# Row sums on VectorE beside the gates and outputs of two more groups, and row tiles spaced by the time that steps leave to transfers

## The chip, the core and the metric

One core of one Trainium2 chip runs the whole program. The metric is the device time of one execution in microseconds. All data are float32.

## What is computed

One layer of a hybrid backbone on 1280 tokens of width 1024: 256 context tokens and 1024 latent tokens. In the kernel they are ten chunks of 128 tokens. Cut to what matters, the layer is:

```python
h = rmsnorm(x) * (1 + sc1) + sh1
u, v, zb, q, k, rv, rg_f, rg_b, gm = split(h @ w_in)
merged = sig(ga) * gmlp(u, v) + sig(gb) * pool(zb) + sig(gc) * retention(q, k, rv, rg_f, rg_b)
x = x + gt1 * (merged @ w_out)
h2 = rmsnorm(x) * (1 + sc2) + sh2
# retrieval: 8 heads, 16 of 16384 experts for each token and head
top_s, top_i = top_k(h2 @ wq . subkeys, 16)      # both sides, then the 16 best of 256 sums
act = gelu(u_tab[expert] . h2);  wgt = softmax(best) * act
x = x + gt2 * sum_over_experts(wgt * v_tab[expert])
y = rmsnorm(x)
```

## The kernel before

**Row tiles.** A token needs 128 experts, so a chunk of 128 tokens needs 16384 of them. They are fetched in row tiles, 128 for each chunk and 1280 in all. A row tile is one indirect transfer, issued by GpSimd (L993), that gathers 128 rows of 8 KB from the table: the u half and the v half of 128 experts, 1 MB together. It fills one of 8 slots (6 at first). Row `R` then goes through the engines:

- VectorE multiplies the u half with the tokens and sums: the dot product (L1558).
- ScalarE, one row later (`ACT_LAG`), makes the gelu (L1033) and the weight (L1036), and scales a small folding matrix by it (`lhs`, L1044).
- TensorE, three rows later (`PE_LAG`), multiplies the v half with that matrix and adds to two banks of PSUM (L1289). The slot is free when this is done.

For *chained* rows the last two steps differ. ScalarE leaves out L1044. VectorE, two rows after the dot product (`VEC_LAG`), scales the v half by the weight and adds the previous row's result (L1570; L1567 for the first row of a run). TensorE takes the last of a run of 16 (`RUN`) only. A chained row's slot is free when VectorE has made the next row's sum, the last one's when TensorE has taken it.

**The other work.** Everything but the row tiles is the *front*, a list of steps in a fixed order. Each step carries a planned cost for TensorE, ScalarE and VectorE. After the modulation, stage 0 and group 0 (context tokens), the list has the retention and pooling of the latent tokens (stage 1), then groups of chunks: `GROUPS = ((0, 1), (2, 3), (4, 5, 6), (7, 8, 9))`. A group's steps are `v` and `u` (products for the spatial gating), `ga` (its gate), `mix`, `rg` and `gc` (retention and its gate), `gb` (pooling's gate), `tr`, `wo` (output product), and `h2a` to `h2c`. A product step is 8 pairs of 128x128 by 512 on TensorE with a planned cost of 7.0. Then comes the group's ranking: `wq` steps on TensorE, and `topa`, `topb`, `topc` steps on VectorE, which find the experts. Some of the `topb` and `topc` steps of a group stand between the `v`, `ga`, `rg` and `gc` steps of the next. In the list the last 35 steps are ranking steps of the last group, 33 of them `top` steps.

Weights come in units of 2 MB from SyncE's queue into two buffers. A step that is the first to use a unit has `ev.first` set. A group has 20 units: 4 for `v` and `u`, 12 from `ga` to `wo`, and 4 for `wq`.

**Placing the row tiles.** All engines read one list, `plan.events`, in which `merge` puts the row tiles between the steps. For each group of rows it takes the stretch of the front from the step that makes them ready to the one that makes the next group's ready, adds up the larger of the planned costs of each step (`wall`), and gives each step a due row in proportion to the sum so far. Row tiles are placed while they are due and ready. The rows of group 0 thus lie beside stage 1, group 1 and the start of its ranking, those of group 1 (256 to 511) beside group 2, and those of group 2 (512 to 895) beside group 3. The last group's rows (896 to 1279) start at the last 35 steps, one for every `LAST_PACE` = 2.9 of `wall`; what is left follows when the front is done, with nothing between. `row_of` and `ready` hold a row back until its experts are ranked: rows 608 and later wait for a step in the middle of group 3's `rg`.

`chains` makes the runs: rows `R` to `R + 15`, with `R` a multiple of 16, if all are placed from the end of group 0's ranking to the first `wq` of group 1. These are 144 rows.

Of the kernel before, what the change touches and what calls it, by code (L numbers as in the profile page):

```python
# [44 lines left out]
ROWS = P  # L45
NR = NC * ROWS
ACT_LAG, VEC_LAG, PE_LAG = 1, 2, 3
RUN = 16
DEEP = 12
RANK_LAG = 3  # L50
LAST_PACE = 2.9
STAGES = ((0, 1), tuple(range(CC, NC)))
GROUPS = ((0, 1), (2, 3), (4, 5, 6), (7, 8, 9))
ORDER = tuple(c for cs in GROUPS for c in cs)
# [45 lines left out]
def row_of(R):  # L100

    p, rr = divmod(R, ROWS)
    pair, g, qq = rr // 32, rr // 16 % 2, rr % 16
    return p, g, pair, pair * 16 + qq, 2 * pair + qq // 8
# [42 lines left out]
class Plan:  # L147
# [231 lines left out]
    def ranking(self, k):  # L379

        cs = GROUPS[k]
        n, pairs = len(cs), 4 * len(cs)
        heads = [(m, hd) for m in range(pairs) for hd in range(2)]
        sides, sums = iter(heads), iter(heads)
        behind = 0

        def top(part, m, hd):
            pair, i = divmod(m, n)
            ev = self.add("top" + part, g=k, i=m, h=2 * pair + hd, j=hd, c=cs[i], p=BASE[k] + i,
                          z=4 * BASE[k] + m, y=self.at["rank", k, m],  # L390
                          act=.8 * (hd == 0 and part == "c") + 2.4 * (hd == 1 and part == "b"), dve=3.0)
            if part == "b" and hd == 1 and m:
                before, ib = divmod(m - 1, n)
                ev.ready = (BASE[k] + ib, before)

        for m in range(RANK_LAG if k else 0):
            self.query(k, m)
            yield
        for m in range(pairs):
            if k and m + RANK_LAG < pairs + 2:  # L400
                self.query(k, m + RANK_LAG)
                yield
            for _ in range(2):
                top("a", *next(sides))
                behind += 1
                yield
                if k == 0 or behind > DEEP - 2:
                    at = next(sums)
                    for part in "bc":
                        top(part, *at)  # L410
                        yield
                    behind -= 1
            if k:
                at = next(sums)
                for part in "bc":
                    top(part, *at)
                    yield
                behind -= 1
        yield "scored"
        for at in sums:  # L420
            for part in "bc":
                top(part, *at)
                yield
        ev = self.add("gsm", g=k, z=4 * BASE[k] + pairs - 1, act=3.2, dve=.2)
        ev.ready = (BASE[k] + n - 1, 3)
        yield
# [39 lines left out]

    def merge(self):

        wall = [max(ev.cost) for ev in self.front]
        starts = [self.ready[BASE[k], int(len(cs) > 2)] for k, cs in enumerate(GROUPS)] + [len(self.front)]  # L470
        due = [0.0] * (len(self.front) + 1)
        for k, cs in enumerate(GROUPS):
            a, b = starts[k], starts[k + 1]
            total = sum(wall[a:b])
            rows = min(len(cs) * ROWS, total / LAST_PACE if k == len(GROUPS) - 1 else len(cs) * ROWS)
            spent = 0.0
            for n in range(a, b):
                spent += wall[n]
                due[n + 1] = BASE[k] * ROWS + rows * spent / total
        self.loaded, self.tail, self.x_at, self.gt_at, row = set(), [], 0, 0, 0  # L480
        placed, first, last = [], None, None
        for n, ev in enumerate(self.front):
            self.events.append(ev)
            self.spare(row, n + 1)
            while row + 1 <= due[n + 1] and self.ready[row_of(row)[0], row_of(row)[2]] <= n + 1:
                self.row(row, n + 1)
                placed.append(n)
                row += 1
            if ev.kind == "wq" and ev.g == 1 and last is None:
                last = n  # L490
            if ev.kind == "gsm" and ev.g == 0:
                first = n
                self.few = -(-(row + 1) // FEW) * FEW
        while row < NR + PE_LAG:
            self.row(row, len(self.front))
            row += 1
        self.chains(placed, first, last)

    def chains(self, placed, first, last):

        self.chained = set()
        for R in range(0, len(placed) - RUN, RUN):
            if placed[R] >= first and placed[R + RUN - 1] < last:
                self.chained.update(range(R, R + RUN))
        self.by_pe, self.by_vec = [0], [0]
        for R in range(NR):
            self.by_vec.append(self.by_vec[-1] + (R in self.chained))
            self.by_pe.append(self.by_pe[-1] + (R not in self.chained or self.chain_end(R)))
# [1441 lines left out]
```

## Time and profile before

| | |
|---|---|
| median of 3 runs | 4773.0 us (4768.74 to 4779.91) |
| the profiled execution, time | 4785.21 us |
| its span | 4783.5 us |
| TensorE busy | 3840.5 us (80%) |
| VectorE busy | 2843.5 us (59%) |
| ScalarE, GpSimd busy | 1638.0, 1617.0 us (34%) |
| moved by DMA | 1687.28 MB, 353 GB/s over the span |
| of it by row tiles | 1342.26 MB |

A share is a mean over stages with different limits, so the stages must be looked at one by one. A busy TensorE is not one at its peak: its clock is granted at one of two levels, and a mean of 0.64 says how the time was divided between them.

### The profile page before, as it was taken

Reading aid. Unit: us, or ns where it says so; the run is one execution under the profiler, and the core shown is the slowest. Engines: PE = TensorE matmul, PEld = TensorE weight load, DVE = VectorE, ACT = ScalarE, POOL = GpSimd, SP = SyncE. Lnnn points to the kernel's source line nnn. Section 1 sums busy time; section 2 is a strip of 40 time slices with the busy share of each in tenths; the row PEclk is TensorE's granted clock in tenths of the full one; section 3 lists DMA queues with packets and bytes.
Section 4 is the critical chain, followed back from the end, with each engine's and each line's share of the span. In section 5 each row is a group of like instructions: output and inputs, shape, how many; then the busy total and the mean of one; then the engine's idle time right before and its main releaser. Section 6 shows DMA issues by size and latency. Waiting matters only on the chain. (4 is left out here: it accounts for less than half of the span.)

```text
span 4783.5 us, 44034 instructions
## 1 busy us (share of the span) xinstructions
PE 3840.5 (80%) x11761; PEld 1567.2 (33%) x11761; DVE 2843.5 (59%) x6525; ACT 1638.0 (34%) x5132; POOL 1617.0 (34%) x1312
## 2 busy tenths in 40 slices
PE   6999799999998869999785897888776456676666
PEld 4645355564444323353331231342222001111110
DVE  1112587566576685754699656545688974544544
ACT  4110254332122343433344433333443443333333
POOL 0000023222222233333343434443333245455454
PEclk8999899999999879999896997999887556666666
DMA  7544688889899989999999999999999789999998
GB/s 260 214 184 185 219 310 311 290 310 355 340 399 394 357 311 398 395 382 382 371 380 343 400 377 384 406 396 407 409 399 382 291 319 421 407 421 415 414 421 351
DMA packets 290057, 1687.28 MB, mean 353 GB/s; under 512 B 29136, under 2 KB 71184, under 8 KB 111120
## 3 DMA queue, kind: packets, MB, share of 16 engines
q0 software_dynamic: 184320, 1342.26, 70.3%
q1 hardware_dynamic: 97472, 318.79, 17.6%
q10 hardware_dynamic: 8016, 23.42, 1.5%
q8 instruction: 94, 1.54, 0.1%
q14 instruction: 155, 1.27, 0.1%
HBM read 1646.57 MB, written 37.78 MB: 352 GB/s over the span
## 5 line engine op out<-in xcount | busy, mean ns | idle before, releaser
L993 POOL DMA_INDIRECT slots<-in_peer,idxR x1280 | 1610.8, 1258 | 3110.6 <-PE ps L1289 1924.3
L1289 PE MATMUL ps<-slots,lhs 128*64 128x512 f32 x4544 | 1523.3, 784 | 736.3 <-ACT lhs L1044 714.9
L1558 DVE CUSTOM_DVE_ANT_0 slots<-slots,h2R 128x1024 f32<-128x1024 f32 x1280 | 1547.6, 1224 | 792.8 <-issue 726.3
L1273 PE MATMUL ps<-ring,arena 128*128 128x512 f32 (+1 forms) x3996 | 1588.8, 555 | 52.1 <-DMA ring<-in_wq 19.0
L1273 PEld LDWEIGHTS ps<-ring,arena 128*128 128x128 f32 x3996 | 767.9, 196 | 894.8 <-issue 819.9
L1289 PEld LDWEIGHTS ps<-slots,lhs 128*64 128x64 f32 x4544 | 297.0, 160 | 1856.1 <-ACT lhs L1044 1596.7
L1033 ACT ACTIVATE gelus<-dots 128x1 f32<-128x1 f32 x1280 | 256.1, 200 | 1525.1 <-DVE dots L1558 1504.1
L1044 ACT ACTIVATE lhs<-fold,wgts 128x64 f32<-128x64 f32 x1136 | 395.0, 348 | 37.2
L1036 ACT ACTIVATE wgts<-gelus,gsmR 128x1 f32<-128x1 f32 x1280 | 377.1, 295 | 42.1
L1273 PE MATMUL ps<-ring,slots 128*128 128x512 f32 (+1 forms) x704 | 249.1, 515 | 0.0
L1570 DVE SCALAR_TENSOR_TENSOR slots<-slots,wgts 128x1024 f32<-128x1024 f32 x135 | 173.1, 1283 | 81.4 <-ACT wgts L1036 75.7
L1273 PEld LDWEIGHTS ps<-ring,slots 128*128 128x128 f32 x704 | 133.5, 190 | 112.4 <-issue 105.0
L1221 ACT ACTIVATE tmp<-ps 128x512 f32<-128x512 f32 x60 | 35.8, 597 | 285.7 <-PE ps L1273 285.7
L1273 PE MATMUL ps<-arena,ring 128*128 128x512 f32 x256 | 115.6, 606 | 17.6 <-DMA arena<-hT_scratch 17.6
L1804 DVE SCALAR_TENSOR_TENSOR tmp<-tmp,ps 128x512 f32<-128x512 f32 x40 | 27.5, 687 | 148.9 <-ACT tmp L1226 148.9
L1558 DVE DVE_READ_ACCUMULATOR2_ANT dots<- 128x1 f32 x1280 | 105.8, 83 | 0.0
L1065 ACT ACTIVATE gsmR<-es,rsum 64x8 f32<-64x8 f32 x320 | 95.1, 297 | 15.5 <-DVE rsum L1635 8.5
L1226 ACT ACTIVATE tmp<-ps 128x512 f32<-128x512 f32 x40 | 23.9, 597 | 189.1 <-PE ps L1273 189.1
L1033 ACT ACT_TABLE_LOAD x59 | 75.7, 1283 | 34.8 <-DVE dots L1558 34.0
L1245 ACT ACTIVATE arena<-ps 128x512 f32<-128x512 f32 x40 | 23.8, 595 | 183.2 <-PE ps L1273 183.2
L1388 PE MATMUL ps<-arena,tmp 128*128 128x256 f32 x160 | 55.1, 429 | 34.7 <-DVEq L1722 19.3
L1273 PEld LDWEIGHTS ps<-arena,ring 128*128 128x128 f32 x256 | 48.5, 193 | 82.7 <-issue 82.6
(197 smaller groups left out, 2344.7 us busy)
## 6 DMA issues: line engine op xcount, KB each, us to landing
ring<-in_whead SPq DMA_DIRECT2D x24, 2048.0 KB
ring<-in_wa SPq DMA_DIRECT2D x24, 2048.0 KB
ring<-in_wq SPq DMA_DIRECT2D x16, 2048.0 KB
slots<-in_peer,idxR POOLq DMA_INDIRECT x1280
ring<-in_wlate SPq DMA_DIRECT2D x16, 1024.0 KB
ring<-in_wgc SPq DMA_DIRECT2D x16, 1024.0 KB
ring<-in_wgb SPq DMA_DIRECT2D x8, 2048.0 KB
ring<-in_wout SPq DMA_DIRECT2D x8, 2048.0 KB
```

The costliest lines, as they stand in the source:

```text
L993: g.indirect_dma_start(out=slot(R), out_offset=None, in_=a["peer"], in_offset=bass.IndirectOffsetOnAxis(ap=idxR[:, p % KEEP, g2, col:col + ...
L1033: st.link(A_(gelus[:, n:n + 1], dots[:, n:n + 1], ACT.Gelu_apprx_tanh))
L1036: weights = A_(wgts[:, n:n + 1], gelus[:, n:n + 1], ACT.Copy, scale=gsmR[:, p % KEEP, g2, col:col + 1])
L1044: A_(lhs[:, n, :], fold[:, :], ACT.Copy, scale=wgts[:, n:n + 1]).then_inc(s["w_done"], 1)
L1065: done = A_(gsmR[i * HALF:(i + 1) * HALF, p % KEEP, g2, h * 8:h * 8 + 8], es[there, z % 2, hd, :].rearrange("p (q i) -> p i q", i=2)[:, i, :],
L1221: A_(tmp[:, ev.x % TMPS, :], bank(t), ACT.Tanh, scale=0.5).then_inc(freed[t % BANKS], 1)
L1273: done = mm(out, lhsT, rhs, start=n == 0, stop=n == len(pairs) - 1)
L1289: done = mm(ps[j * HALF:(j + 1) * HALF, g2, :], weights, slot(R)[:, D + j * UW:D + (j + 1) * UW], start=start, stop=stop)
L1388: mm(out, sm[:, ev.i % 2, r * P:(r + 1) * P], vv[ev.g][:, cs[r], :], start=True, stop=False)
L1558: v.tensor_tensor_reduce(out=u, in0=u, in1=h2R[:, g2, :], scale=1.0, scalar=0.0, op0=ALU.mult, op1=ALU.add, accum_out=dots[:, R % LHS:R % ...
L1570: v.scalar_tensor_tensor(out=here, in0=here, scalar=wgts[:, n:n + 1], in1=slot(R - 1)[:, D:2 * D], op0=ALU.mult, op1=ALU.add).then_inc(s[" ...
L1804: v.scalar_tensor_tensor(out=gate, in0=gate, scalar=1.0, in1=bank(t), op0=ALU.add, op1=ALU.mult).then_inc(freed[t % BANKS], 1)
```

## The change

The rows' due times follow another measure. `spare_time` runs two clocks through the front, TensorE's and VectorE's, with the planned costs, and lets neither run more than `AHEAD` = 20 ahead of the other. A step's spare time is what it adds to the later of the two clocks, less `UNIT_TIME` = 5.3 if it is the first to use a weight unit. The last group's rows are placed at one for every `ROW_TIME` = 1.5 of spare time. The planned VectorE cost of a `top` step goes from 3.0 to 3.2. And `chains` takes runs in two more stretches: from the first `ga` to the last `wo` of groups 2 and 3.

```diff
-LAST_PACE = 2.9
+ROW_TIME, UNIT_TIME, AHEAD = 1.5, 5.3, 20.0
...
-                          act=.8 * (hd == 0 and part == "c") + 2.4 * (hd == 1 and part == "b"), dve=3.0)
+                          act=.8 * (hd == 0 and part == "c") + 2.4 * (hd == 1 and part == "b"), dve=3.2)
...
-        wall = [max(ev.cost) for ev in self.front]
         starts = [self.ready[BASE[k], int(len(cs) > 2)] for k, cs in enumerate(GROUPS)] + [len(self.front)]
+        spare = self.spare_time()
...
-            total = sum(wall[a:b])
-            rows = min(len(cs) * ROWS, total / LAST_PACE if k == len(GROUPS) - 1 else len(cs) * ROWS)
+            total = sum(spare[a:b])
+            rows = min(len(cs) * ROWS, total / ROW_TIME if k == len(GROUPS) - 1 else len(cs) * ROWS)
             spent = 0.0
             for n in range(a, b):
-                spent += wall[n]
+                spent += spare[n]
                 due[n + 1] = BASE[k] * ROWS + rows * spent / total
...
-        self.chains(placed, first, last)
-
-    def chains(self, placed, first, last):
+        stretches = [(first, last)]
+        for k in range(2, len(GROUPS)):
+            mine = [n for n, ev in enumerate(self.front) if ev.g == k and ev.kind in ("ga", "wo")]
+            stretches.append((mine[0], mine[-1]))
+        self.chains(placed, stretches)
+
+    def spare_time(self):
+
+        pe = dve = clock = 0.0
+        spare = []
+        for ev in self.front:
+            pe, dve = pe + ev.cost[0], dve + ev.cost[2]
+            pe, dve = max(pe, dve - AHEAD), max(dve, pe - AHEAD)
+            spare.append(max(pe, dve) - clock - UNIT_TIME * ev.first)
+            clock = max(pe, dve)
+        return spare
+
+    def chains(self, placed, stretches):
...
-            if placed[R] >= first and placed[R + RUN - 1] < last:
+            if any(a <= placed[R] and placed[R + RUN - 1] < b for a, b in stretches):
                 self.chained.update(range(R, R + RUN))
```

## Rows read from the trace of the kernel before

**Rows 1.** The page: the span, and the span in 40 equal slices.
```profile
span 4783.5 us, 44034 instructions
...
PEclk8999899999999879999896997999887556666666
DMA  7544688889899989999999999999999789999998
GB/s 260 214 184 185 219 310 311 290 310 355 340 399 394 357 311 398 395 382 382 371 380 343 400 377 384 406 396 407 409 399 382 291 319 421 407 421 415 414 421 351
```

**Rows 2.** Busy time by stretch; the first line names the columns, POOL counts row tiles.
```profile
core 0: us, PE busy (x) PEld busy (x) DVE busy (x) ACT busy (x) POOL busy (x), PEclk, DMA share, GB/s
573.00:1557.00 984.00, 895.77 (x2894) 493.16 (x2896) 664.42 (x1312) 304.51 (x981) 261.80 (x227) 0.96 0.88 336
1557.00:1765.00 208.00, 150.98 (x456) 57.13 (x452) 164.59 (x539) 73.13 (x219) 57.99 (x51) 0.80 0.89 330
1660.00:1765.00 105.00, 62.94 (x172) 19.40 (x172) 98.05 (x331) 42.54 (x128) 32.55 (x27) 0.69 0.83 303
1765.00:1888.00 123.00, 119.54 (x344) 44.98 (x346) 74.81 (x160) 49.19 (x152) 47.07 (x39) 1.00 0.98 400
1888.00:2265.00 377.00, 362.35 (x1138) 156.15 (x1136) 218.08 (x434) 131.56 (x417) 143.30 (x107) 0.99 0.97 383
2265.00:2639.00 374.00, 264.90 (x826) 94.67 (x824) 312.55 (x954) 159.45 (x479) 129.88 (x113) 0.82 0.93 365
2540.00:2639.00 99.00, 56.38 (x138) 13.18 (x136) 91.53 (x287) 44.73 (x135) 28.80 (x28) 0.64 0.88 324
2639.00:2809.00 170.00, 151.93 (x432) 51.53 (x430) 99.47 (x200) 65.21 (x215) 72.14 (x59) 0.93 0.99 407
2809.00:3330.00 521.00, 443.92 (x1362) 173.53 (x1358) 294.65 (x571) 180.83 (x586) 213.80 (x165) 0.92 0.97 390
3330.00:3730.00 400.00, 292.09 (x908) 99.79 (x908) 301.58 (x833) 166.44 (x525) 154.24 (x139) 0.78 0.98 399
3730.00:3880.00 150.00, 65.50 (x142) 10.96 (x140) 142.24 (x444) 74.51 (x213) 40.03 (x35) 0.52 0.74 256
4000.00:4700.00 700.00, 473.42 (x1090) 73.29 (x1088) 346.75 (x563) 238.20 (x830) 386.64 (x273) 0.64 1.01 416
```

**Rows 3.** The gates' first use (L1785) and outputs' end (L1844), groups 2 and 3.
```profile
L1785 DVE SCALAR_TENSOR_TENSOR arena<-tmp,arena x6: 691/692/693, 1888.2 to 1941.0; 128x512 f32<-128x512 f32 x6
...
L1844 DVE TENSOR_TENSOR arena<-arena,inb x6: 691/692/693, 2217.8 to 2260.1; 128x512 f32<-128x512 f32 x6
...
L1785 DVE SCALAR_TENSOR_TENSOR arena<-tmp,arena x6: 692/693/693, 2808.8 to 2858.6; 128x512 f32<-128x512 f32 x6
...
L1844 DVE TENSOR_TENSOR arena<-arena,inb x6: 691/692/693, 3273.3 to 3327.1; 128x512 f32<-128x512 f32 x6
```

**Rows 4.** Waits from 4000 to 4700 us: total, times, longest.
```profile
POOL slots L993 <- PE ps L1289: 251.8, 143, 4.3
```

**Rows 5.** TensorE's time for row tiles (L1289 alone), by stretch, columns as before.
```profile
1888.00:2265.00 377.00, 106.48 (x434) 26.48 (x432) 0.99 0.97 383
...
3730.00:3880.00 150.00, 64.18 (x134) 9.77 (x132) 0.52 0.74 256
```

**Rows 6.** Costliest groups of VectorE: busy us, mean ns, idle before.
```profile
L1558 DVE CUSTOM_DVE_ANT_0 slots<-slots,h2R 128x1024 f32<-128x1024 f32 x1280 | 1547.6, 1224 | 792.8 <-issue 726.3 <-DMA slots<-in_peer,idxR 44.9 <-DVE ti L1578 8.3
L1570 DVE SCALAR_TENSOR_TENSOR slots<-slots,wgts 128x1024 f32<-128x1024 f32 x135 | 173.1, 1283 | 81.4 <-ACT wgts L1036 75.7 <-DVE arena L1734 2.8 <-DVE tmp L1720 1.9
```

**Rows 7.** Waits from 1888 to 2265 us.
```profile
POOL slots L993 <- PE ps L1289: 213.4, 51, 7.9
```

**Rows 8.** GpSimd's row tile issues from 941 to 1550 us, then from 1888 to 2270 us.
```profile
L993 POOL DMA_INDIRECT slots<-in_peer,idxR x136 | 161.8, 1190 | 450.7 <-DVE slots L1570 414.8 <-PE ps L1289 23.3 <-issue 12.6
...
L993 POOL DMA_INDIRECT slots<-in_peer,idxR x109 | 145.4, 1334 | 239.3 <-PE ps L1289 213.4 <-issue 25.6 <-DVE idxR L1623 0.3
```

**Rows 9.** Waits from 941 to 1550 us, with the chained rows.
```profile
DVE slots L1570 <- ACT wgts L1036: 71.0, 27, 4.5
```

## The prediction

> **What bounds the kernel now.** I read the page's slices first [rows 1]. From the sixth slice on the DMA engines are busy nine tenths of the time or nearly, with a dip at slices 32 and 33. When the front is done, nothing but row tiles is left, and their 1 MB transfers run at a share of 1.01 and 416 GB/s: 273 in 700 us, 2.56 us each (the last row of [rows 2]). GpSimd waits there for slots [rows 4], but the transfers that fill them are what takes the time. So 2.56 us is the price of a row tile wherever transfers bind, and total bytes don't change. A gain can only come from stretches where the DMA engines idle.
>
> So I cut the span at the front's steps: the gates' and outputs' places [rows 3] give four edges, the row tiles' counts the others, and the busy times by stretch [rows 2] show what binds each:
> - 573 to 1557 (stage 1, group 1): TensorE, 896 of 984 us; DMA share 0.88.
> - 1660 to 1765, 2540 to 2639 and 3730 to 3880, the ends of the rankings, where `top` steps stand alone: VectorE, 93, 92 and 95% busy. DMA falls to 0.83, 0.88 and 0.74.
> - 1765 to 1888 (`v`, `u` of group 2): TensorE, 97%.
> - 1888 to 2265 (gates to outputs, group 2): TensorE 96% and DMA 0.97 together.
> - 2639 to 3730: DMA, 0.97 to 0.99. TensorE has 85% from gates to outputs.
>
> **The change: where rows go.** The planned costs, summed over the steps, give the due row at each edge. By `wall`, group 2's stretch of the list has 733 (2.86 a row), group 3's 721 (1.88); by spare time 433 (1.69) and 428 (1.11). A group's `v` and `u` have 110 of `wall`, but only 43 of spare time: 84 of TensorE, less 4 units of 5.3, and less 20 that VectorE is ahead after the ranking. From gates to outputs it is 306 to 312 against 209. The last 35 steps have 103.4 / 2.9 = 36 rows before and 33 x 3.2 = 105.8 / 1.5 = 71 after.
>
> Rows in each stretch, before then after: stage 1 and group 1, 230 then 241; ranking to 1765, 48 and 47; `v`, `u` to 1888, 39 and 25; gates to outputs to 2265, 107 and 123; to 2639, 113 and 119; `v`, `u` to 2809, 58 and 39; to 3330, 166 and 187; to 3730, 135 and 115; last 35 steps, 36 and 71; left over, 348 and 313. The counts of issues [rows 2] follow the first numbers within 4.
>
> **The last 35 steps.** VectorE is 142 of 150 us busy with 35 rows placed, and DMA at 0.74 [rows 2]. A dot product is 1.22 us alone, 1.15 from start to start with its read (1547.6 / 1280 is 1.21; I take 1.2) [rows 6]. 35 more rows make 150 + 35 x 1.2 = 192 us for 71 rows, 2.7 a row: just over a transfer's 2.56, so VectorE still binds and DMA is nearly full. TensorE's row products took 64 us for 34 rows at a granted clock of 0.52 [rows 5], so 71 need 134 of 192: hidden. Leftover rows: 35 fewer at 2.56, -90. Sum: +42 - 90 = **-48 us**. If each added row costs nothing, it is -90 (VectorE had only 8 us idle, so no); if each costs a transfer, 0.
>
> **The chains.** Rows 320 to 431 and 608 to 767 lie wholly in the new stretches: 112 and 160 chained rows; and 11 more rows lie in the old one, which makes one more run. For each, TensorE loses 106.5 us / 108 rows = 1.0 us [rows 5] (but for one row in 16), ScalarE 0.35 us, and VectorE gets 1.28 us [rows 6] (a run's first row is a plain scaling, which I bound by the same price).
> - Gates to outputs, group 2. TensorE: 362 - 107 + 18 = 273 us. VectorE: 218 + 16 x 1.2 + 112 x 1.28 = 381. DMA: 0.97 x 377 + 16 x 2.56 = 407. Transfers bind; at the same share of 0.97, 420 us, **+43**.
> - Group 3. TensorE: 444 - 160 + 21 = 305. VectorE: 295 + 25 + 205 = 525. DMA: 505 + 54 = 559; at 0.97, 577 us, **+56**.
>
> So chaining by itself is worth about nothing: transfers were at 0.97 there. Slots come free otherwise: GpSimd waited for TensorE's row products 213 us of 377, up to 7.9 at once [rows 7], behind steps of 7 us, and now waits for VectorE, whose steps are 3.3 us or less. The bound upwards is a share of 1.0 as in rows-only time: -13 and -17. I take 0.
>
> The Trainium skill (SBUF — State Buffer, Who interferes with whom) says that a VectorE instruction with two SBUF inputs contends with a GpSimd instruction that reads SBUF; L1570 is one. In the stretch that has chains, an issue took 1190 ns, in the one without 1334 [rows 8], so the trace doesn't show it; what it would do is a rival below.
>
> **The other stretches.**
> - `v`, `u` of group 2: 14 fewer unchained rows at 1.0 us of TensorE: **-14**. Group 3: DMA 0.99 x 170 - 19 x 2.56 = 119, but TensorE 152 - 19 = 133, so TensorE becomes the bound, at about 135: **-35** (between -49 and -19).
> - To 2639: 6 more rows fit in transfers' idle 7% (26 us); 7 us of VectorE beside 312 of 374: **+3**. The dip at the end goes, as more rows stand by the `top` steps, but VectorE's total is the same.
> - To 3730: 20 fewer rows, DMA 392 - 51 = 341, VectorE 302 - 24 = 278: 355 us, **-45**.
> - To 1557: TensorE binds, 11 more chained rows cost it under 1 us, and fit in DMA's idle 118 us: **0**. To 1765: **0**.
>
> **Sum:** 0 + 0 - 14 + 43 + 3 - 35 + 56 - 45 - 48 = **-40**. The profiled execution has 4785.2 us, 12 above the median of 4773.0; the same difference from the median gives **4733 us**. The middle of the kernel comes out at +8; the gain is the end's. About 0.2% (10 us) is what a measurement can tell from no change.
>
> **Rivals.**
> 1. *VectorE becomes the bound from gates to outputs (slower).* It will have 381 of 420 and 525 of 577 us, 91%. A chained row's sum waits for its weight from ScalarE: in the old stretch 71 us over 136 rows, 0.52 each [rows 9]. There it cost nothing, as TensorE bound. If VectorE waits as much now, 272 rows make 142 us: 381 + 58 = 439 and 525 + 84 = 609, which is 51 over my 997, and the kernel ends at 4784. It decides from a busy share of 906 / 1037 = 87% for VectorE: above, I gain, below, I don't. For it: in-order engines. Against: ScalarE was late there because it waited for TensorE's products, and TensorE now has a third of its time free. VectorE has reached 93 to 95% elsewhere [rows 2].
> 2. *The middle gains too.* If all from 1557 to 3730 runs at a DMA share of 1.0, the idle time goes: 2173 us before, of which transfers take 2085 (each stretch's length by its DMA share); minus 11 rows (28 us) is 2057, against my 2181 (+8). That is 124 us better; half of it, with 4671 us, is this rival. For it: slots freed by VectorE in small steps, and the dips at 0.83 and 0.88. Against: `v`, `u` will be bound by TensorE, and rows 608 on still wait in a bunch.
> 3. *The end gives nothing.* The 35 rows lengthen the ranking by a transfer's time each, since each dot product now waits for its row: -48 becomes 0 or so, in all 4775. Against: VectorE's idle time in that stretch is 8 us, so rows came before they were asked for.
> 4. *Chains slow the issues.* If each chained sum and dot product blocks GpSimd, a row needs 1.33 + 1.28 + 1.22 = 3.8 us of it: 310 rows make 1190 us against 997: 4926. The trace speaks against it [rows 8]. By the page named above it would need GpSimd reading SBUF during most of an issue.
>
> TensorE's clock: from gates to outputs it was at 0.99 and 0.92 of full, with TensorE 96 and 85% busy; in 3330 to 3730 with 73% busy, 0.78 [rows 2]. With 273 and 305 us of work in 420 and 577 I expect 0.75 to 0.85, so the work takes up to 364 and 407 us: still hidden. The Trainium skill (TensorE: Matmul & The Clock Gate, HAM oscillation) has it that gaps between bursts bring the slow level back; the rows agree, and it changes nothing unless TensorE stays at half speed throughout (546 us in 420). That would be a form of rival 1.
>
> **Chances.** Forecast (4700 to 4763) 0.47; rival 2, 0.21; rival 3 and mixtures near no change, 0.13; rival 1, 0.17; rival 4, 0.02. Faster by over 0.2%: the first two and a little of the third's mixtures, 0.70; same 0.13; slower 0.17. The range takes in half of the middle's gain and rival 1's price: 4655 to 4787; the forecast's own is 4700 to 4763.
>
> **What would show it.** The last `top` steps about 190 us long with some 70 rows, DMA above 0.9; 35 fewer rows after the front. L1570 in three places, x405 or so. From gates to outputs of groups 2 and 3: 420 and 577 us, VectorE 91% busy, DMA 0.97, TensorE's row products down to a few us, PEclk 0.75 to 0.85. `v`, `u`: 110 and 135 us. It is wrong if VectorE's waits for L1036 in these stretches pass 50 us (rival 1), if the stretches run at a DMA share of 1.0 (rival 2), or if the leftover rows start no earlier than before in the count (rival 3).

## The result, and the profile after

The changed kernel takes 4831.0 us (median of 4 runs, 4826.8 to 4836.2), the kernel before beside it 4776.5. The ratio is 1.011, with a 95% interval of 1.0096 to 1.0125: slower by 55 us, where the forecast was 40 faster. It lies above the range, whose upper end is 4787.

The page of the changed kernel, the span and its 40 slices, which answers to [rows 1]:

```profile
span 4829.2 us, 42108 instructions
...
PEclk8999899999999879887888897776887766666666
DMA  7554588899898887899979999999998999999998
GB/s 257 214 187 181 196 309 307 320 330 393 340 376 345 319 320 317 354 364 412 397 305 373 377 384 360 368 398 416 405 397 323 403 397 399 407 421 415 415 421 352
```

The dip at slices 32 and 33 has gone, as forecast. There are new ones: slices 13 to 16 (the end of group 1, its ranking, and `v` and `u` of group 2) run at 317 to 345 GB/s, and slices 21 and 31, beside rankings, at 305 and 323.

Busy time by stretch, cut at the same steps as in [rows 2], with the same columns:

```profile
591.00:1599.00 1008.00, 893.05 (x2861) 491.75 (x2860) 679.55 (x1307) 302.75 (x987) 282.83 (x237) 0.95 0.88 336
1599.00:1809.00 210.00, 147.72 (x433) 57.12 (x432) 167.56 (x540) 71.86 (x215) 52.89 (x49) 0.77 0.85 320
1809.00:1916.00 107.00, 107.00 (x295) 41.71 (x293) 58.66 (x132) 37.87 (x111) 26.76 (x25) 1.00 0.77 304
1916.00:2340.00 424.00, 286.41 (x774) 142.09 (x772) 362.87 (x575) 106.40 (x348) 142.36 (x121) 0.83 0.95 378
2340.00:2739.00 399.00, 276.95 (x862) 99.63 (x861) 324.29 (x972) 163.83 (x503) 135.81 (x122) 0.82 0.93 367
2739.00:2874.00 135.00, 124.45 (x345) 46.08 (x345) 74.03 (x157) 48.00 (x152) 39.72 (x38) 0.96 0.88 353
2874.00:3460.00 586.00, 314.07 (x848) 147.59 (x844) 504.04 (x780) 150.50 (x502) 217.72 (x184) 0.76 0.97 388
3460.00:3821.00 361.00, 262.89 (x828) 94.85 (x828) 274.95 (x788) 143.96 (x456) 138.12 (x122) 0.82 0.93 375
3821.00:4004.00 183.00, 108.01 (x272) 21.40 (x272) 174.21 (x493) 98.54 (x303) 69.36 (x66) 0.66 1.00 395
4100.00:4700.00 600.00, 403.05 (x932) 62.92 (x928) 298.64 (x485) 204.40 (x710) 319.26 (x233) 0.64 1.01 416
```

The profiled execution before ended at 4783.5, this one at 4829.2: 46 later. Stretch by stretch, the forecast and what came of it, in us:

| Stretch | rows before, after (planned) | forecast | measured |
|---|---|---|---|
| to the end of group 1 | 230, 241 | 0 | +42 (18 of it before the first row) |
| ranking, then `v` and `u` of group 2 | 48, 47; 39, 25 | 0; -14 | +2; -16 |
| gates to outputs, group 2 | 107, 123 | +43 | +47 |
| `h2` and ranking | 113, 119 | +3 | +25 |
| `v` and `u`, group 3 | 58, 39 | -35 | -35 |
| gates to outputs, group 3 | 166, 187 | +56 | +65 |
| `h2` and ranking to row 896 | 135, 115 | -45 | -39 |
| last 35 steps and what follows | 384, 384 | -48 | -45 |
| sum | | -40 | +46 |

Each is the stretch's length or its end, taken from the lines above and from [rows 2]; the last is 4829.2 - 3821 against 4783.5 - 3730. The two `v`, `u` stretches and the end came out to a few us. The loss is in the first line and in four lines that each came out 4 to 22 us worse than forecast. Of the four only the 22 us (`h2` and ranking) is more than two traces of the same work can differ by, about 10 us (see e13 and e14).

Of the first line, 18 us come before any row: in the changed list the first row stands six steps further on in the front (step 169, counted from 0, instead of 163).

Who waited in the changed kernel from gates to outputs, first of group 2 (1916 to 2360 us), then of group 3 (2874 to 3483): total, times, longest.

```profile
PE ps L1304 <- DVE slots L1585: 92.2, 6, 32.8
```

```profile
PE ps L1304 <- DVE slots L1585: 230.0, 9, 36.9
```

TensorE waits 322 us at run ends, 15 times, up to 37 us at once. It looks like a cause; e7 and e8 test it.

The costliest groups of the changed kernel with the chained sum (L1585, before L1570):

```profile
L1008 POOL DMA_INDIRECT slots<-in_peer,idxR x1280 | 1540.8, 1204 | 3227.4 <-PE ps L1304 1514.4
...
L1585 DVE SCALAR_TENSOR_TENSOR slots<-slots,wgts 128x1024 f32<-128x1024 f32 x405 | 518.2, 1280 | 68.6 <-ACT wgts L1051 59.0
```

405 sums, as counted. They waited for ScalarE's weights 59 us in all, and in the two new stretches no such wait of L1585 is left; rival 1 had 142 us. An issue takes 1204 ns on average with three times as many chained sums; in the kernel before it took 1258 ns. Rival 4 is out. The Trainium skill (SBUF — State Buffer, Who interferes with whom) has it that a VectorE instruction with two SBUF inputs contends with a GpSimd instruction that reads SBUF; in these issues no such contention is seen.

### The profile page after: what moved, and what is told of

Same layout as the page of the kernel before. It is cut to its first block and busy times, and to the rows that moved or that the text cites. A ratio compares the mean times of both kernels' runs of the same rounds, so it can differ in the third digit from the quotient of the medians.

```text
span 4829.2 us, 42108 instructions
## 1 busy us (share of the span) xinstructions
PE 3566.9 (74%) x10681; PEld 1522.6 (32%) x10681; DVE 3166.6 (66%) x6813; ACT 1534.4 (32%) x4837; POOL 1547.1 (32%) x1312
## 5 line engine op out<-in xcount | busy, mean ns | idle before, releaser
L1008 POOL DMA_INDIRECT slots<-in_peer,idxR x1280 | 1540.8, 1204 | 3227.4 <-PE ps L1304 1514.4
L1304 PE MATMUL ps<-slots,lhs 128*64 128x512 f32 x3392 | 1193.3, 817 | 586.6 <-ACT lhs L1059 570.3
L1288 PEld LDWEIGHTS ps<-ring,arena 128*128 128x128 f32 x3996 | 781.3, 198 | 961.9 <-issue 874.0
L1304 PEld LDWEIGHTS ps<-slots,lhs 128*64 128x64 f32 x3392 | 229.4, 168 | 1476.7 <-ACT lhs L1059 1294.2
L1585 DVE SCALAR_TENSOR_TENSOR slots<-slots,wgts 128x1024 f32<-128x1024 f32 x405 | 518.2, 1280 | 68.6 <-ACT wgts L1051 59.0
L1059 ACT ACTIVATE lhs<-fold,wgts 128x64 f32<-128x64 f32 x848 | 294.9, 348 | 27.8
L1304 PE MATMUL ps<-slots,fold 128*64 128x512 f32 x108 | 45.3, 931 | 337.6 <-DVE slots L1585 337.6
L1236 ACT ACTIVATE tmp<-ps 128x512 f32<-128x512 f32 x60 | 35.5, 592 | 231.6 <-PE ps L1288 230.6
L1774 DVE TENSOR_TENSOR inb<-ps,inb 128x512 f32<-128x512 f32 x20 | 13.8, 691 | 106.6 <-PE ps L1288 98.2
```

What stands on the lines that cost most here:

```text
L1008: g.indirect_dma_start(out=slot(R), out_offset=None, in_=a["peer"], in_offset=bass.IndirectOffsetOnAxis(ap=idxR[:, p % KEEP, g2, col:col + ...
L1059: A_(lhs[:, n, :], fold[:, :], ACT.Copy, scale=wgts[:, n:n + 1]).then_inc(s["w_done"], 1)
L1236: A_(tmp[:, ev.x % TMPS, :], bank(t), ACT.Tanh, scale=0.5).then_inc(freed[t % BANKS], 1)
L1288: done = mm(out, lhsT, rhs, start=n == 0, stop=n == len(pairs) - 1)
L1304: done = mm(ps[j * HALF:(j + 1) * HALF, g2, :], weights, slot(R)[:, D + j * UW:D + (j + 1) * UW], start=start, stop=stop)
L1585: v.scalar_tensor_tensor(out=here, in0=here, scalar=wgts[:, n:n + 1], in1=slot(R - 1)[:, D:2 * D], op0=ALU.mult, op1=ALU.add).then_inc(s[" ...
```

## The experiments

Four kernels first, to part the spacing from the chains. Times are medians, ratios are to the kernel before on the same chip, with the 95% interval. The runs were made on several chips, on which the kernel before had medians of 4773 to 4778 us, so a difference of a few us between two experiments says nothing.

**e1, the new spacing without the new chains.**

```diff
         stretches = [(first, last)]
-        for k in range(2, len(GROUPS)):
-            mine = [n for n, ev in enumerate(self.front) if ev.g == k and ev.kind in ("ga", "wo")]
-            stretches.append((mine[0], mine[-1]))
```

> The changed kernel without the chains beside groups 2 and 3 (160 chained rows, all beside stage 1 and group 1); the spacing is the changed one. Theory S, the spacing loses: chains are nearly free, the time stays within 10 us of the changed kernel's 4831. Theory V, the chains make VectorE the bound and TensorE waits at run ends (332 us of waits for L1585 in the two stretches): without them gates to outputs run at the pace of transfers, 425 and 580 us where the changed kernel has 444 and 609, and the time is 4785 to 4800.

Measured 4809.7 us, ratio 1.0072 (1.0052 to 1.0092). It lies between the two theories' numbers: the spacing loses 34 us by itself (by the ratio), and the chains beside groups 2 and 3 the other 21.

**e2, the new chains without the new spacing.** The lines that e1 takes away are put into the kernel before.

> The kernel before with the new chains alone (384 chained rows), rows spaced by the larger planned cost as before. Theory S: within 10 us of before, 4776. Theory V: slower by 20 to 50 us, in the stretches from gates to outputs (before 394 and 551 us up to the last h2b), with VectorE at 85 to 90% and DMA below 0.95 there.

Measured 4801.2 us, ratio 1.0058 (1.0039 to 1.0077): the chains cost 28 us here. Theory V has the time; whether VectorE's load is the cause is a second question, for e8. From gates to outputs of group 2, e2 and then the kernel before, cut alike:

```profile
1884.00:2281.00 397.00, 290.62 (x810) 143.52 (x806) 339.43 (x549) 112.81 (x347) 134.29 (x112) 0.87 0.95 376
```

```profile
1888.00:2282.00 394.00, 372.09 (x1172) 160.25 (x1168) 230.46 (x454) 146.52 (x445) 148.70 (x112) 0.98 0.97 384
```

TensorE loses 81 us of work and the stretch doesn't shrink: VectorE is 85% busy instead of 58%, the transfers' share falls from 0.97 to 0.95, and TensorE's granted clock from 0.98 to 0.87. The two traces differ by 12 us at their ends, 3 of them in this stretch.

**e3, the new spacing for the last group alone.** `merge` takes `spare` for the last group and `wall` for the others; no new chains (a `top` step keeps its new cost of 3.2).

```diff
+            cost = spare if k == len(GROUPS) - 1 else wall
-            total = sum(spare[a:b])
+            total = sum(cost[a:b])
...
-                spent += spare[n]
+                spent += cost[n]
```

> The kernel before with one edit: the last group's rows at one for 1.5 of spare time (70 beside the last 35 steps where before had 36). Both theories: the end gained 45 us in the changed kernel (+41 in the last steps, -86 after them), and nothing else moves, so 4731, faster than both. If the end's gain needs the other edits, 4776.

Measured 4744.3 us, ratio 0.9942 (0.992 to 0.9965): 29 us faster than before, and the first version that beats both. It is less than the 45 of the traces; the profiled execution of before was itself 12 us above its median.

**e4, the changed kernel with the first 256 rows spaced as before** (`cost = spare if k > 0 else wall`).

> The changed kernel, but rows 0 to 255 spaced by the larger planned cost as before (230 instead of 241 by the end of group 1). The changed kernel reached the end of group 1 at 1599 us, 42 later than before. Theory S, these 42 us are lost for good because more chained rows stand beside the retention steps: 4790 to 4805. Theory V, most of it is given back, as 11 rows more must then be placed later at 2.56 us each (28 us): 4815 to 4825.

Measured 4810.0 us, ratio 1.0073 (1.0053 to 1.0092): 21 us of the loss are the first rows' (with the one run of chains less that the old spacing makes there). It lies between the two theories' numbers.

**e5, e3 and group 2 spaced by spare time** (`cost = spare if k in (1, len(GROUPS) - 1) else wall`).

> The version with only the end spaced anew (4744), and rows 256 to 511, beside group 2, spaced by spare time as well. No new chains. With the changed spacing and no new chains, rows 256 to 511 took 924 us where before had 877; rows 512 to 895 took 1179 and 1173. Theory P (a row's price depends on what binds: 1.0 us where TensorE binds, 1.2 where VectorE binds, 2.56 where transfers bind): rows leave v and u at 1.0 each and arrive from gates to outputs at 2.56, so most of the 47 us are here: 4780 to 4791. Rival, the loss is spread over all groups by bytes and chance: 4744 to 4760.

Measured 4786.0 us, ratio 1.0019 (1.0004 to 1.0034). Against e3 that is 42 us, where the new spacing of all rows lost 34 with the end's 29 gained. The parts add up: -29 for the end, +42 for group 2, +21 for the first rows make +34, so group 3's spacing costs about nothing, to within some 17 us (an estimate from the intervals of e1, e4, e5 and the changed kernel).

**e6, e3 with ranking's `top` steps weighing 1.5 times** in groups 2 and 3.

```diff
+        heavy = [max(ev.cost) * (1.5 if ev.kind[:3] == "top" else 1.0) for ev in self.front]
...
-            cost = spare if k == len(GROUPS) - 1 else wall
+            cost = spare if k == len(GROUPS) - 1 else heavy if k else wall
```

> The version with only the end spaced anew (4744), and in groups 2 and 3 the planned cost of ranking's top steps counts 1.5 times for the spacing, so 7 to 13 rows of each group go from gates and outputs to the ranking. Theory P: they cost 1.2 us where VectorE binds alone and save 2.56 where transfers bind: 15 to 25 us faster, 4720 to 4730. Rival, every row costs a transfer wherever it is: 4744.

Measured 4740.4 us, ratio 0.9911 (0.9882 to 0.994). By the medians that is 4 us from e3, by the ratios 15, and the two intervals overlap. So a gain isn't shown, and a small one isn't excluded; the median lies outside the 4720 to 4730 of theory P.

**e7, e2 with TensorE's last row of a run taken 3 rows later**, so that it stands behind VectorE by more.

```diff
-                    if 0 <= ev.i - PE_LAG < NR and plan.on_pe(ev.i - PE_LAG):
-                        row(ev.i - PE_LAG)
+                    R = ev.i - PE_LAG
+                    if 0 <= R < NR and plan.on_pe(R) and not plan.taken_late(R):
+                        row(R)
+                    if plan.taken_late(R - LATE):
+                        row(R - LATE)
```

> The kernel with the new chains alone (4801), but TensorE takes a run's last row 3 row tiles later in its order, except where the bank is read next. Theory W, the chains cost time because TensorE waits at run ends (297 us of waits for the chain's sum in groups 2 and 3) and is late for the products after it: most of the 28 us comes back, 4775 to 4785. Theory V, VectorE's own load (86% busy from gates to outputs) is the cost: 4795 to 4805.

Measured 4798.3 us, ratio 1.0038 (1.0027 to 1.005), 3 us from e2. `taken_late` holds for 9 of the 15 new run ends only: not for those with no chained row behind them, nor for the last row of a bank. From gates to outputs of group 2, TensorE's wait for the chain's sum fell from 86.6 us, the first line below (e2), to 45.2, the second (e7):

```profile
PE ps L1293 <- DVE slots L1574: 86.6, 5, 27.6
```

```profile
PE ps L1298 <- DVE slots L1582: 45.2, 4, 20.3
```

In group 3 it fell from 210.2 to 180.6 us. So about a quarter of 297 us of waits went, and the time fell by 3 us (by 6, taken against the kernel before on each chip). If the cost went with the length of the waits, a quarter of 28 us would be 7. The median is theory V's, but e7 took away too little to refute theory W.

**e8, e2 in runs of 8** (`RUN = 8`).

> The kernel with the new chains alone (4801), in runs of 8 instead of 16, so that there are twice as many run ends for TensorE to wait at and VectorE's load is the same (392 chained rows). Theory W: the waits double in number, 4815 to 4835. Theory V: 4795 to 4805, or a few us less, since each wait is shorter.

Measured 4839.7 us, ratio 1.013 (1.0103 to 1.0156): 38 us slower than e2, for 25 more runs. TensorE's waits in the same stretch are twice as many, and the total is hardly more (1894 to 2315 us). Below them, the stretch itself:

```profile
PE ps L1293 <- DVE slots L1574: 93.3, 11, 15.0
```

```profile
1894.00:2315.00 421.00, 308.49 (x836) 147.61 (x832) 336.44 (x549) 113.46 (x347) 130.66 (x113) 0.86 0.90 356
```

VectorE has 336 us of work where e2 had 339, and the transfers' share fell from 0.95 to 0.90. So a run end has a price, 1.5 us each on average, which VectorE's load doesn't explain; nor does the total length of TensorE's waits, which grew by 7 us here. It isn't the same everywhere: this stretch grew by 24 us for 6 more run ends, group 3's by 14 (574 for 560) for 10 more. Theory W had the time right. By which way a run end costs stays open.

At 1.5 us each (an estimate from e8), the 15 new run ends of e2 make 23 of its 28 us, and the 17 of the changed kernel make 26, where the chains cost 21. So the run ends alone come near to the whole cost of the chains, and little is left for VectorE's load.

**e9, e5 with the rows spread evenly inside.** The rows at the edges of group 2's stages are e5's; from gates to outputs they are spread in proportion to `wall`.

```diff
             cost = spare if k == len(GROUPS) - 1 else wall
+            if k == 1:
+                mine = [n for n, ev in enumerate(self.front) if ev.g == 2 and ev.kind in ("ga", "wo")]
+                c, d = mine[0], mine[-1] + 1
+                share = sum(spare[c:d]) / sum(wall[c:d])
+                cost = spare[:c] + [share * x for x in wall[c:d]] + spare[d:]
```

> As the version with the end and group 2 spaced by spare time (4786): the same rows at every edge of group 2's stages (287 at v, 312 at the first gate, 436 at the end of the outputs), but from gates to outputs they are spread by the larger planned cost, evenly, not by spare time. There 16 more rows cost 57 us in that version, 3.5 each, where transfers would take 41. Theory E, the rest is unevenness inside (1 row beside a step that loads a unit, 4 beside the others): 4765 to 4775. Theory P, the counts at the edges decide: 4786.

Measured 4754.8 us, ratio 0.9953 (0.9938 to 0.9969): 31 of the 42 us come back. From gates to outputs, e5 and then e9:

```profile
1897.00:2347.00 450.00, 395.94 (x1232) 163.92 (x1228) 247.50 (x483) 158.89 (x489) 173.32 (x127) 0.96 0.95 375
```

```profile
1894.00:2308.00 414.00, 381.11 (x1230) 162.50 (x1226) 247.97 (x483) 155.95 (x486) 166.62 (x128) 0.99 1.00 407
```

One issue more in 36 us less: transfers at 1.00 instead of 0.95, and 407 GB/s instead of 375. GpSimd's longest wait for a slot that TensorE frees fell from 12.1 to 9.4 us, the total from 259 to 228. TensorE's waits for the weights of row tiles halve (e5, then e9, in the same stretches):

```profile
PE ps L1303 <- ACT lhs L1058: 44.0, 31, 2.5
```

```profile
PE ps L1308 <- ACT lhs L1063: 22.9, 15, 3.0
```

**e10, the opposite: e3's rows at the edges, spread by `spare` from gates to outputs of group 2** (the same edit with `spare` and `wall` exchanged).

> The opposite: the version with only the end spaced anew (4744), the same rows at every edge of the stages as there (317 at the first gate, 422 at the outputs' end), but from gates to outputs of group 2 spread by spare time. Theory E: 4755 to 4765. Theory P: 4744.

Measured 4758.5 us, ratio 0.9956 (0.994 to 0.9973): by the medians 14 us slower than e3, as theory E has it, by the ratios 7, and the intervals overlap. With no rows added unevenness costs less; that it costs at all here is likely, and not shown.

**e11, e6 with a denser end** (`ROW_TIME = 1.2`, 87 rows beside the last 35 steps).

> The version with the end spaced anew and heavier top steps (4740), the last group's rows at one for 1.2 of spare time, so that 87 stand beside the last 35 steps, not 70. At 70 the transfers there are at 0.99 to 1.00. By prices, 17 rows more need 44 us of transfers in a stretch of 183 that is full, and leave 44 us after it: 4740. If VectorE still set the pace there (1.2 us a row): 4717.

Measured 4730.4 us, ratio 0.9892 (0.9869 to 0.9915), 10 us below e6, between the two numbers, with intervals that overlap. Its last 35 steps take 213 us, with transfers at 1.01:

```profile
3735.00:3948.00 213.00, 132.05 (x338) 26.34 (x339) 195.31 (x529) 111.73 (x353) 88.78 (x83) 0.69 1.01 417
```

**e12, e6 with chains from `v` to the first `rg` of group 2**, 80 rows more.

> The version with the end spaced anew and heavier top steps (4740), with chains from v to the first rg of group 2 (rows 288 to 367, 80 more), where TensorE is 97% busy and VectorE 60%. TensorE loses 75 us of row products in 240. If TensorE's load is what holds these steps: 4715 to 4730. If transfers at 0.93 to 0.98 are: 4740.

Measured 4751.3 us, ratio 0.9939 (0.9923 to 0.9956), 11 us slower than e6 and above both numbers. Even where TensorE was 97% busy, taking row products from it gave nothing. The transfers had a share of 0.93 there (e6's trace, 1784 to 2160 us).

**e13, e1 spread evenly inside every stage, and e14, the changed kernel spread in the same way.** The rows at the edges of the stages stay those of the changed kernel (at the last `top` step 964 for 966).

```diff
-        spare = self.spare_time()
+        spare = self.even(self.spare_time(), [max(ev.cost) for ev in self.front])
...
+    def even(self, spare, wall):
+        edges = [0] + [self.ready[BASE[k], int(len(cs) > 2)] for k, cs in enumerate(GROUPS)] + [len(self.front)]
+        for kind, g in (("on", 1),) + tuple((kind, g) for g in (1, 2, 3) for kind in ("v", "ga", "h2a")):
+            edges.append(next(n for n, ev in enumerate(self.front) if ev.kind == kind and ev.g == g))
+        out = []
+        edges = sorted(set(edges))
+        for a, b in zip(edges, edges[1:]):
+            share = sum(spare[a:b]) / sum(wall[a:b])
+            out += [share * x for x in wall[a:b]]
+        return out
```

> The changed spacing without the new chains (4810), with the same rows at the edges of all stages (125 at the end of the retention, 184, 238, 287, 312, 436, 555, 593, 781, 896), but spread inside each stage by the larger planned cost. Theory E, unevenness inside the stages is the cost of the new spacing: group 2 gives back 31 us as measured alone, and the first rows' 21 come back too: 4755 to 4765. If the first rows' loss is the edges': 4775 to 4785.

> The changed kernel (4831) with its rows spread evenly inside the stages in the same way, new chains included. Theory E with the chains' cost added as measured (21 to 28 us): 4780 to 4795, so still slower than before. If uneven rows are what made the chains cost: 4755 to 4765.

e13 measured 4729.3 us, ratio 0.9901 (0.9879 to 0.9924): 80 us faster than e1, more than the 50 expected, and 48 faster than before. e14 measured 4755.3 us, ratio 0.9957 (0.994 to 0.9973): 76 us faster than the changed kernel, and faster than before. e14 has the number of the second theory, but only because smoothing gave more than I had reckoned: the chains cost 26 us between e14 and e13, as much as in e1 and e2, so unevenness is not what makes them cost.

The two kernels also show how far single traces agree. Up to the gates of group 2 they do the same work in the same order, and these gates start at 1886 us in e13 and at 1876 us in e14. So stretches of two traces that differ by less than 10 us are not told apart.

Stretches of e1, then of e13, cut at the same steps (to the first `v` of group 1, to its end, to the first gate of group 2, to its end, to the first gate of group 3, to its end, to row 896):

```profile
590.00:1322.00 732.00, 658.26 (x2251) 375.39 (x2250) 504.10 (x1056) 254.01 (x839) 220.18 (x183) 0.96 0.86 327
1322.00:1600.00 278.00, 236.03 (x609) 117.69 (x608) 174.75 (x250) 48.62 (x148) 62.74 (x54) 0.91 0.91 356
1600.00:1915.00 315.00, 251.93 (x727) 97.42 (x725) 226.38 (x673) 110.02 (x327) 79.69 (x74) 0.85 0.83 317
1915.00:2364.00 449.00, 392.65 (x1230) 163.15 (x1228) 248.03 (x484) 158.50 (x487) 167.00 (x127) 0.97 0.95 375
2364.00:2879.00 515.00, 392.50 (x1170) 141.92 (x1170) 385.30 (x1109) 198.37 (x627) 170.39 (x155) 0.85 0.91 362
2879.00:3472.00 593.00, 484.03 (x1486) 182.42 (x1482) 339.33 (x643) 220.32 (x693) 236.80 (x191) 0.91 0.98 399
3472.00:3809.00 337.00, 252.79 (x788) 91.75 (x788) 260.52 (x764) 129.57 (x422) 129.03 (x114) 0.82 0.93 372
```

```profile
567.00:1303.00 736.00, 665.94 (x2279) 379.11 (x2280) 518.32 (x1113) 255.62 (x845) 214.88 (x183) 0.96 0.89 333
1303.00:1567.00 264.00, 234.10 (x611) 117.21 (x609) 177.88 (x253) 49.77 (x151) 65.08 (x55) 0.94 0.93 373
1567.00:1886.00 319.00, 253.03 (x726) 97.65 (x726) 222.92 (x670) 109.68 (x324) 80.70 (x73) 0.88 0.85 321
1886.00:2297.00 411.00, 381.42 (x1234) 162.01 (x1230) 249.17 (x486) 160.44 (x493) 170.72 (x129) 0.99 1.00 405
2297.00:2789.00 492.00, 382.23 (x1166) 137.94 (x1168) 382.81 (x1107) 196.76 (x623) 168.34 (x152) 0.88 0.95 380
2789.00:3396.00 607.00, 495.96 (x1498) 186.47 (x1494) 340.66 (x650) 223.31 (x702) 259.74 (x194) 0.89 0.97 390
3396.00:3718.00 322.00, 242.83 (x784) 87.87 (x780) 256.17 (x756) 126.45 (x416) 125.97 (x111) 0.82 0.97 396
```

Row 896 comes at 3718 instead of 3809, 91 us earlier. 23 of them are the first row's start (567 for 590; it stands seven steps earlier in the front); then come 14 in group 1, 38 in group 2 from gates to outputs, 23 to the first gate of group 3 and 15 in its ranking. Two stretches give 4 each back, and group 3 from gates to outputs gives 14 back, with more issues in it (194 for 191). TensorE's work is 2656 us over these stretches for 2668, and VectorE's hardly differs: what went is the transfers' idle time, in group 2 from 0.95 to 1.00 and after it from 0.91 to 0.95. So smoothing helps in sum, and a gain isn't seen in every stage.

## Why the prediction was wrong

- **The step that failed** is the treatment of a stretch as one sum: rows times a price, under the largest of three loads. It gave 0 for the stretch to 1557 ("11 more chained rows cost it under 1 us, and fit in DMA's idle 118 us"), which measured +42, and +3 for the stretch to 2639 ("6 more rows fit in transfers' idle 7%"), which measured +25. I worked out how many rows lie in each stretch by spare time, but not how they lie from step to step, which the same formula gives: one beside a step that first uses a unit, four or five beside each of the next two. With the very counts that I priced, spread evenly, the kernel takes 4729 us (e13), against 4810 spread by spare time (e1), both without the new chains; with them it is 4755 (e14) against 4831. That is shown. The counts by themselves are thus worth 48 us (e13 against the kernel before), near the 40 that I had forecast for them. The reason why bunched rows idle the transfers is argued, not shown: 8 slots hold 8 rows, and the engines take rows in the order of the list; TensorE's waits for row weights (44 against 23 us) and GpSimd's for slots (259 against 228) point to it.
- **Chains.** "Chaining by itself is worth about nothing" failed too: it costs 21 (changed kernel against e1), 28 (e2) and 26 us (e14 against e13). My loads were right (VectorE 381 and 525 us forecast, 363 and 504 in the stretches measured; TensorE 273 and 305 against 286 and 314). Gates to outputs took 424 and 586 us for my 420 and 577. So VectorE was 86% busy, below the 87% that I had named as rival 1's point. Rival 1 had the sign, with 51 us for it, and not the mechanism: the chained sums hardly wait for their weights. The term that I left out is the run end, where TensorE takes VectorE's sum: e8 shows a price of 1.5 us each on average, which for 17 new ones comes to the chains' whole cost. How it works is open, and a cost of VectorE's load by itself is not shown.
- **What was right.** The end: 183 us for the last steps against 192, DMA at 1.00, and 45 us gained in the trace against 48; alone it is worth 29 (e3). `v` and `u`: -16 and -35 against -14 and -35. In the first TensorE is at its bound, busy 107 of 107 us; in the second it is busy 124 of 135, where I had 133. TensorE's clock: 0.83 and 0.76 for my 0.75 to 0.85. The Trainium skill (TensorE: Matmul & The Clock Gate, HAM oscillation) has it that gaps between bursts bring the slow level back; the trace agrees.
- **Rivals.** 2 did not happen in this kernel: the transfers' idle time moved to `v` and `u` (0.77 and 0.88). 3 is refuted by e3 for the end. 4 is refuted by the issues' 1204 ns.
- **Price of rows.** The price of 1.2 against 2.56 us a row was tried in e6 for a small move: 15 to 25 us expected, 4 measured by the medians and 15 by the ratios. It is undecided.

## What to carry to other kernels

A schedule has two scales: how many transfers lie in a stage, and how they lie from step to step. Here the first was worth 48 us and the second 80 (e1 to e13), so a measure that fits the stage totals must still be smoothed over a few steps when the buffers hold no more than that. And relieving an engine that is 97% busy gave nothing where the transfers were nearly as busy (0.97 in e2's stretch, 0.93 in e12's), although the engine that took the load had 40% of its time to spare. The cost was near what the added run ends make at e8's 1.5 us each, so longer runs are what I would try next; no kernel here had them.

## What the runs showed of the hardware

The transfers' mean busy share hides a difference of rate. From gates to outputs of group 2, share 0.95 went with 375 GB/s and 1.00 with 407 (e5, e9), in rows-only time 1.01 with 416. There the step from 0.95 to 1.00 was worth 8%, not 5. It is no fixed rate: in the last 35 steps of the changed kernel a share of 1.00 went with 395 GB/s.

TensorE's granted clock fell from 0.98 to 0.87 when most of its row products left it in e2. What was left hardly took longer. The products of the front from gates to outputs of group 2, in e2 (1884 to 2281 us) and in the kernel before (1888 to 2282 us), have the same count and 252 us each:

```profile
L1277 PE MATMUL ps<-ring,arena 128*128 128x512 f32 x464 | 208.0, 609 | 10.5 <-ACT arena L1233 9.7 <-DMA ring<-in_whead 0.8
L1277 PE MATMUL ps<-ring,arena 128*128 128x256 f32 x192 | 44.0, 392 | 0.0
```

```profile
L1273 PE MATMUL ps<-ring,arena 128*128 128x512 f32 x464 | 209.1, 604 | 0.8 <-ACT arena L1229 0.8
L1273 PE MATMUL ps<-ring,arena 128*128 128x256 f32 x192 | 43.0, 382 | 0.0
```

So the lower mean clock was not a loss here: TensorE's work fell by 81 us, and its row products alone by 85 (113 to 28).
